# Output projection of a pooling and convolution layer: the pool half as four groups of seven block products, and the pool map moved into the input projection

## The reference, cut to what matters

```python
proj = h @ w_in                      # 2048 -> 4096: u | B | C | v, 1024 each
u, bg, cg, v = ...
ya, new_pool = _pool_mixer(pool_prev, u, pos0, w_pool, pool_scale)
#   per group g (256 channels, window 2/4/8/16):
#   d = mean over the window - u;  y = (d @ w_pool[g]) * pool_scale
yb, new_conv = _conv_mixer(conv_prev, bg, cg, v, conv_w)     # B * conv3(C * v)
x = x + jnp.concatenate([ya, yb], axis=-1) @ w_out           # 2048 -> 2048
x = x + _cross_attn(...)             # 4 heads over 256 memory tokens
x = x + square(relu(rms(x) @ w_up)) @ w_down
```

## Time and profile before

| what | value |
|---|---|
| median of 3 runs | 2573.04 us (2572.37 to 2573.59) |
| the profiled execution | 2572.41 us, of it span 2570.7 us |
| PE busy | 2542.2 us, 99% of the span, 19628 matmuls |
| DVE busy | 2018.9 us, 79% |
| ACT busy | 1162.8 us, 45% |
| share of PE in the chain that ended last | 90% |
| share of DVE in it | 6% |
| granted TensorE clock | 0.998 of full speed |

### The profile page before, as it was taken

How to read it: one execution, slowest core, us unless ns; L and a number is a source line. 1 busy time by engine, 2 the same in 40 slices (tenths; PEclk the granted TensorE clock), 3 DMA queues, 4 the chain that set the end, 5 groups by cost and what they waited for, 6 DMA issues and landing times.

```text
span 2570.7 us, 46979 instructions
## 1 busy us (share of the span) xinstructions
PE 2542.2 (99%) x19628; PEld 2476.8 (96%) x19628; DVE 2018.9 (79%) x2510; ACT 1162.8 (45%) x1616; POOL 174.7 (7%) x278
## 2 busy tenths in 40 slices
PE   8999999999999999999999999999999999999998
PEld 7889999999999979899999999999999999999997
DVE  8898888763686663478888888888888888888888
ACT  6445444441453341245555555666543333333344
POOL 1000000010000020000111110000010000000000
PEclk9999999999999999999999999999999999999999
DMA  8663333362334385433566665555586565556532
GB/s 306 208 206 123 108 106 110 118 221 87 132 125 161 123 323 206 172 117 109 178 223 220 225 222 212 195 190 206 203 306 219 192 227 209 208 191 224 195 129 103
DMA packets 134499, 471.44 MB, mean 183 GB/s; under 512 B 12544, under 2 KB 18816, under 8 KB 123040
## 3 DMA queue, kind: packets, MB, share of 16 engines
q1 hardware_dynamic: 92224, 259.74, 30.4%
q0 software_dynamic: 41664, 208.62, 21.9%
q10 hardware_dynamic: 416, 0.30, 0.0%
HBM read 381.08 MB, written 87.54 MB: 182 GB/s over the span
## 4 chain that ended last, share of the span: by engine, by line
PE 90%; DVE 6%; issue 2%; ACT 2%; DMA 1%; DVEq 0%; ACTq 0%; POOL 0%; POOLq 0%; SPq 0%
PE psum_main L2915 27%; PE psum_side L2915 20%; PE psum_main L2501 14%; PE psum_main L2629 10%; PE psum_side L2629 8%; PE psum_main L2605 3%; PE psum_main L2558 2%; DVE unit_low L2159 1%; PE psum_main L2839 1%; PE psum_main L2767 1%; PE psum_main L2560 1%; DMA unit_raw<-weights 1%; ACT unit_high L1335 1%; PE psum_side L2808 1%; PE psum_side L2708 1%
## 5 line engine op out<-in xcount | busy, mean ns | idle before, releaser
L1335 ACT ACTIVATE unit_high<-unit_raw 128x1024 fp32r<-128x1024 f32 x382 | 398.6, 1055 | 520.2 <-PE psum_main L2915 159.0
L2159 DVE TENSOR_TENSOR unit_low<-unit_raw,unit_high 128x1024 fp32r<-128x1024 f32 x382 | 465.5, 1222 | 101.7 <-ACT unit_high L1335 101.5
L2915 PE MATMUL psum_main<-tokens_late,unit_high 128*128 128x272 f32 x2048 | 388.5, 288 | 2.0 <-DVE hidden L2261 1.0
L2915 PE MATMUL psum_main<-hidden,unit_high 128*128 128x272 f32 x1984 | 376.8, 288 | 0.7 <-DVE residual_late L2293 0.7
L2915 PEld LDWEIGHTS psum_main<-tokens_late,unit_high 128*128 128x128 f32 x2048 | 321.9, 189 | 2.6 <-DVE hidden L2261 1.5
L2915 PEld LDWEIGHTS psum_main<-hidden,unit_high 128*128 128x128 f32 x1984 | 312.2, 189 | 1.1 <-DVE residual_late L2293 0.9
L2915 PE MATMUL psum_main<-tokens_late,unit_low 128*128 128x272 f32 x1024 | 295.1, 288 | 0.0
L2915 PE MATMUL psum_side<-tokens_late,unit_high 128*128 128x272 f32 x1536 | 293.1, 288 | 1.5 <-issue 0.8
L2629 PE MATMUL psum_main<-tokens,unit_high 128*128 128x272 f32 x1536 | 292.1, 288 | 0.9 <-DVE pool_lines L1713 0.7
L2915 PE MATMUL psum_main<-hidden,unit_low 128*128 128x272 f32 x992 | 286.1, 288 | 0.0
L2915 PE MATMUL psum_side<-hidden,unit_high 128*128 128x272 f32 x1488 | 283.6, 288 | 0.0
(11 more groups left out here) (339 smaller groups left out, 5044.8 us busy)
## 6 DMA issues: line engine op xcount, KB each, us to landing
unit_raw<-weights SPq DMA_DIRECT2D x436, 512.0 KB, 4.3
hidden<-hidden_kept POOLq DMA_DIRECT2D x56, 1088.0 KB, 5.7
hidden_kept<-hidden_staged POOLq DMA_DIRECT2D x31, 1904.0 KB, 7.4
unit_sum<-weights SPq DMA_DIRECT2D x44, 512.0 KB, 3.6
residual<-x_t POOLq DMA_DIRECT2D x16, 544.0 KB, 7.0
residual_kept<-residual_new POOLq DMA_DIRECT2D x32, 272.0 KB, 2.3
cache_ring_q<-cache_k POOLq DMA_DIRECT2D x8, 1024.0 KB, 5.9
cache_low_a<-cache_v POOLq DMA_DIRECT2D x8, 1024.0 KB, 10.8
```

What stands on the lines that cost most here:

```text
L1335: act.activation(WHI[:, slot, :], raw, ACT.Copy).then_inc(mlp_high, 1)
L2159: dve.tensor_tensor(WLO[:, slot, :], raw, WHI[:, slot, :].bitcast(F32), ALU.subtract) \
L2915: ins = pe.matmul(bank, w[:, slot, col:col + P], moving[:, k, part, :], start=start and k == 0 and n == 0, stop=k == kk - 1 and n == 2, sk ...
```

## The change

- **The pool half of the output projection** becomes four quads, 16 to 19 (`OUT_QUADS`), of seven products each, with the pool rows as the token side. One product is again 24 matmuls (2 output blocks x 4 inner blocks x 3). Results are not copied: seven DVE additions into X per quad (`add_out`). The quads take their raw blocks as halves of stored units, so each block is two DMAs with 128 numbers (512 bytes) in a run.
- **The token side** of these products needs seven combinations of the pool rows. They are made group by group inside the input projection (`mix_parts`, `low_raw_parts`, `low_mixed_parts` on DVE, `high_raw_parts`, `high_mixed_parts` on ACT), written to DRAM (`parts_kept`) and read back as `PAIRS` into the places of the token operands that quad 15 frees. The last group's are made inside quad 15 and written directly (`high_last_part`, `low_part`).
- **The pool map** of each group runs on PE right behind the value quad (`map_pool`, 24 matmuls), from operands that ACT and DVE split there (`high_differences`, `high_map`, `low_differences`, `low_map`); its results are scaled by ACT in the gate quad (`map_scaled`).
- **The conv rows** keep only two rows on chip (`Y`), are stored per group (`y_kept`) and come back late for the conv half (`high_rows`, `low_rows`).
- Slots of later stages are renumbered, since 18 units leave the ring; the first loads of quad Q0 and of the MLP's quad 0 are issued in another order.

The diff, cut:

```diff
-    ("pool_map", 2,  8,  8, 0, 0,  0),
-    ("pool_out", 16, 16, 0, 0, 0,  0),
+    ("pool_map", 0,  0,  8, 0, 0,  0),
-SLOT_OF = (2, 3, 0, 1, 2, 3, 0)
+SLOT_OF = (0, 1, 2, 3, 0, 1, 2)
+OUT_QUADS = 4
-Q0 = MIX_QUADS
+Q0 = MIX_QUADS + OUT_QUADS
+OUT_ROWS = ((10, 12), (4, 6), (0, 2), (14, 8))
...
@@ SP
+            def load_block(q, tile, w, landed):
+                if not MIX_QUADS <= q < Q0:
+                    sp.dma_start(tile, w).then_inc(landed, 16)
+                else:
+                    for u in range(2):
+                        sp.dma_start(tile[:, u * 512:u * 512 + 512].rearrange("p (g n) -> p g n", g=HK), w[u]) \
+                            .then_inc(landed, 16)
...
@@ POOL
+                if g:
+                    store_parts(g - 1, 3, PRODUCTS, MIXED_PARTS)
+                    store_rows(g - 1)
...
+            for i in range(PRODUCTS):
+                pool.wait_ge(in_used, in_use(last_mix, i // 2))
+                pool.dma_start(PAIRS[i // 2][:, i % 2, 0:3, :, :]..., parts_kept[PART_AT[i]]...)
...
@@ ACT, in the loop over the mixing quads
                 high_in(q, 5)
+                if kind(q) == "pool":
+                    high_mixed_parts(g - 1)
+                if kind(q) == "value":
+                    high_differences(g)
                 act.wait_ge(in_dve, 3 * q + 1)
                 copy_in(q, 3, 0, S[:, 2, 0:HALF])
+                if kind(q) == "value":
+                    high_map(g)
+                if q == MIX_QUADS - 1:
+                    act.wait_ge(mixed, PARTS_MIXED)
+                    high_last_part(PAIRS[1][:, :, 3, 0, :], 1, halves(DIFF[:, 0, :]))
+                    high_last_part(PAIRS[2][:, 0, 3, 0, :], 2, DIFF[:, 1, HALF:TOK])
+                    high_last_part(PAIRS[3][:, 0, 3, 0, :], 3, DIFF[:, 1, 0:HALF])
                 high_in(q, 6)
...
@@ DVE, in the same loop
                 sum_in_4(q)
+                if kind(q) == "pool" and g:
+                    mix_parts(g - 1)
+                if kind(q) == "gate" and g < 3:
+                    low_raw_parts(g)
+                if q == MIX_QUADS - 1:
+                    low_part(done + 1, PAIRS[0][:, :, 3, 1, :], ...)
...
                 low_in(q, 5)
+                if kind(q) == "value":
+                    low_differences(g)
+                if kind(q) == "pool" and g:
+                    low_mixed_parts(g - 1)
+                if q == MIX_QUADS - 1:
+                    low_part(done + 2, ...)
+                    mix_parts(g)
                 low_in(q, 6)
+                if q == MIX_QUADS - 1:
+                    low_part(done + 3, ...)
+                    low_part(done + 4, ...)
+                    low_part(done + 5, ...)
...
+                sum_in_1(q + 1)
+                if q:
+                    block_out(q, 2)
+                low_in(q + 1, 0)
+                if kind(q) == "value":
+                    low_map(g)
+                block_out(q, 3)
...
@@ DVE, quads 16 to 19
+                add_out(q, 3)
+                low_in(q, 6)
+                if q + 1 < Q0:
+                    sum_in_1(q + 1)
+                add_out(q, 4)
+                if q > MIX_QUADS + 1:
+                    for n in range(4):
+                        low_rows(4 * (q - MIX_QUADS - 2) + n)
...
@@ PE
+            def product_out(q, i, out, start):
+                pe.wait_ge(in_ready, in_use(q, i))
+                for m in range(2):
+                    for k in range(HK):
...
+                        for n, (w, part) in enumerate(((WHI, 0), (WHI, 1), (WLO, 0))):
+                            ins = pe.matmul(out[:, m, :], w[:, slot, col:col + P], PAIRS[i // 2][:, i % 2, k, part, :], ...)
+            for q in range(MIX_QUADS, Q0):
...
+                pe.wait_ge(in_dve, done + 1)
+                product_out(q, 2, chain_out(q), False)
...
-            down("pool_out", A, ready_by(psum_free, lambda k: s0["tiles"] + max(5, k + 1)), apart=True)
-            down("conv_out", B, ready_by(y_split, lambda k: k + 1))
+            down("conv_out", B, None, apart=True)
```

More of the change, by code:

```diff
@@ L480, in first_half @@
         def first_half(q, row):
[L482 removed]
             at_line = lambda t, pad: t[:, row, pad:pad + HALF]
[L484 removed]
+            return {"pool": at_line(U, PAD), "content": Y[:, row, 0:HALF], "value": at_line(Z, CPAD),
                     "gate": GATE[:, row, 0:HALF]}[kind(q)]
@@ new lines, in load_map, with store_parts @@
+            def load_map(g):
+                if g:
+                    pool.wait_ge(map_high, 3 * g)
+                    pool.wait_ge(map_ready, 3 * g)
+                pool.dma_start(MAP_RAW[:, :], weights[MAP_IN + g // 2][:, g % 2 * 512:g % 2 * 512 + 512]) \
+                    .then_inc(map_loaded, 16)
+            def store_parts(g, first, last, made):
+                pool.wait_ge(stage_ready, GROUP_PARTS * g + made)
+                pool.dma_start(parts_kept[first:last, :, g].rearrange("i p s n -> p i (s n)"),
+                               PARTS_OUT[:, 0:last - first, :, :].bitcast(F32).rearrange("p i s n -> p i (s n)")) \
+                    .then_inc(parts_stored, 16)
@@ new lines, in _ @@
+            pool.wait_ge(stage_high, PARTS)
+            pool.wait_ge(stage_ready, PARTS)
+            load_x(2)
+            load_x(3)
+            store_rows(3)
+            load_x(0)
+            load_x(1)
+            load_x(7)
+            for n in range(2):
+                pool.wait_ge(k_stored[n], KEYS_STORED + 16 * 4)
+            load_x(4)
+            for n in range(2):
+                pool.wait_ge(in_used, in_use(last_mix, 4 + n))
+                pool.dma_start(B[:, 4 * n:4 * n + 4, 1, :].bitcast(F32),
+                               y_kept[4 * n:4 * n + 4].rearrange("k p n -> p k n")).then_inc(y_back[n], 16)
@@ L1154, in _ @@
-            for c in range(CH):
-                act.wait_ge(y_made, c + 1)
-                act.activation(B[:, c, 0, :], Y[:, c, :], ACT.Copy).then_inc(y_high, 1)
+            for n in range(RING):
+                convert_first(n)
             def down(name, extra=0, groups=4):
@@ L1707, in block_out @@
                     dve.wait_ge(pool_kept, 2 * g + 2)
-                if kind(q) == "gate":
-                    dve.wait_ge(k_stored[row], KEYS_STORED + 16 * (g + 1))
+                if kind(q) == "gate" and g:
+                    dve.wait_ge(y_made, 2 * g)
+                if kind(q) == "content" and g:
+                    dve.wait_ge(k_stored[row], KEYS_STORED + 16 * g)
                 def add(out, a, b):
@@ L1721, in block_out @@
                 elif half:
-                    out = (Y[:, 2 * g + row, :] if kind(q) == "content" else GATE[:, row, :])[:, HALF:TOK]
+                    out = (Y if kind(q) == "content" else GATE)[:, row, HALF:TOK]
                     add(out, bank, part).then_inc(in_dve, 1)
@@ L2529, in down @@
                 if apart:
-                    for j in range(2):
-                        multiply(unit(name, extra, j), j, tiles, 0, True, True, ready if j == 0 else None)
                     group(0, (2, 3))
@@ L2701, in keys_of_caches @@
+            for j in range(2):
+                pe.wait_ge(in_dve, dve_reads(Q0 - 1 + j))
+                multiply(unit("conv_out", 0, j), j, B, 0, True, True, (lambda k: pe.wait_ge(y_split, k + 1)) if j == 0 else None)
+            down("conv_out", B, None, apart=True)
             def keys_of_caches(h, n):
```

563 lines of the change are left out of this document (335 added, 228 removed).

## The result

The changed kernel takes **2587.9 us** (median of 4 runs, 2587.5 to 2588.5) against 2572.7 us (4 runs) of the kernel before on the same chip: ratio 1.006, 95% interval 1.0048 to 1.0071. It is 15 us slower, where 2569.2 us was forecast and the range ended at 2579.5. The span of the profiled execution is 2586.8 us (2570.7 before).

The account below looks back on a forecast made before the run. PE, busy 99% of the span, was taken to bound the kernel; 13.4 us removed against 9.6 us of new waits gave 3.8 us faster, from 2573.04 to 2569.2 us, range 2562.5 to 2579.5.

Parts of the forecast that it names:

- PE's list: Map and pool half on PE: 13.4 us removed, 12.0 from 96 matmuls fewer and 1.4 from waits in the old stage.
- value quads: Quads 2, 6, 10, 14: product 6 waits for block_out, 1.4 us in group 0, 0.5 in group 1; sum 1.9.
- pool quads: Quads 4, 8, 12: mixing on DVE delays block_out, so product 6 waits 0.5 us, three times 1.5 us in all.
- gate quads 3, 7, 11: The parts' low halves come ahead of the taps; taken as nothing, with 0.5 us each as upper bound.
- quad 15: DVE's list: Last parts, mixing and low halves ahead of block_out(15, 2) make product 6 of quad 15 wait 5.0 us.
- quad 16: list: DVE's queue after quad 15 makes product 2 wait 0.6 us and product 4 wait 0.1; sum 0.7.
- quads 16 to 19: weights: Waits for weight blocks in the output quads: 0.5 us in all.
- load term: Weight loads in output quads: nothing up to twice the 4.3 us landing; 0.5 us in all taken.
- rival 2: Output quads wait for weights at sum_in_1 in quads 16 to 18: 10.5 us instead of 0.5, 2579.2 us; chance 0.11.
- The mixing: Pool quads: four DVE operations, each waiting for the last, 0.47 us apart, 1.8 us; 1.4 by the Trainium skill's page.
- the 12 that the prediction named as its sign: PE waiting more than 12 us in all between 230 and 560 us would mean the forecast is too fast.
- rival 3: Content quads of groups 1 to 3 wait for stored conv rows, 1.6 us each: 2574.0; chance 0.12 including other waits.

Follow-up runs that it names:

- i: Changed kernel with each weight block of the output quads stored as one unit, one 512 KB transfer with 4 KB a row: 2574.5 us.
- k: As i, one transfer a block, but the two blocks of a pair of units stored interleaved, so runs are 512 bytes again: 2588.4 us.
- f_best: Changed kernel with a, b and the order of d in every quad: 2573.3 us.
- e_all: Changed kernel with the edits of a, b and d together: 2578.4 us.
- d: Changed kernel; in quad 15 ACT rounds operand 6 before the last parts, DVE does block_out(15, 2) right behind low half 6: 2589.2 us.
- m: Changed kernel with the seven loads of the parts read in runs of 544 bytes, as two transfers each: 2592.9 us.
- b: Changed kernel with the loads of residual and conv rows each behind a product of its own in quads 17 to 18: 2578.7 us.
- a: Changed kernel with the seven loads of the parts spread over nine products instead of four: 2579.4 us.
- c: Changed kernel with the output quads' blocks in the same two halves but in runs of 2 KB (other weights): 2581.1 us.
- g: e_all with the output quads' blocks read in the 2 KB runs of c (other weights): 2572.5 us.
- j: f_best with the whole stored blocks of i: 2566.1 us.
- l: As j, without the spreading of parts and rows (a and b): 2568.1 us.

## Why the prediction was wrong

Counted at the first conv addition; each forecast is the prediction's, each measured number from the profiled execution:

| Term | forecast us | measured us |
|---|---|---|
| PE's list | -13.4 | -13.4 |
| start of the first quad | 0 | +1.2 |
| value quads | +1.9 | +2.4 |
| pool quads | +1.5 | +2.9 |
| gate quads 3, 7, 11 | 0 | +0.9 |
| quad 15: DVE's list | +5.0 | +5.4 |
| quad 15: weights | 0 | +3.3 |
| quad 15: slow clock | 0 | +1.7 |
| quad 16: list | +0.7 | +0.4 |
| quads 16 to 19: weights | +0.5 | +10.1 |
| quad 16: slow clock | 0 | +2.0 |
| not placed | | +1.0 |
| sum | -3.8 | +17.9 |

**The step that failed** is the load term, "Bounds: nothing, if it takes up to twice 4.3, and rival 2 above. ... I take 0.5 us in all, near the lower end, as both rows are". It measured 13.4 us of waits (3.3 + 10.1). The slow clock behind the waits cost 3.7 more; the part in quad 15 (1.7) would largely be there without the late weights too: behind the wait of 5.3 in i, product 6 still takes 4.45 us instead of 3.0 (549.57 to 554.02 us).

Three things in it were wrong. The landing time was taken from rows of quiet stretches and doubled at most; it became 14.2 us for half a block. The only place looked at was quads 16 to 18, while the first late block is the one of quad 16 that is loaded in quad 15, beside the parts. And the row held against rival 2, that 1 KB runs cost 0.3 us more, says nothing of the weights' queue: it is two loads on POOL's queue, and there the runs of 1 KB travel in packets of 4.1 KB (115 packets with 0.47 MB from 958 to 960 us before, with no weights beside them). On SP's queue each run of 512 bytes is a packet.

Against rival 2 stood also a rule of the Trainium skill, page "DMA: Bandwidth & Descriptors", section "Specifications": 512 bytes is the least run for the full rate. The trace does not agree. Nearly alone on full engines (98% of the bytes from 549 to 553 us are the weights'), the runs of 512 bytes move 299 GB/s; alone in the kernel before, in runs of 4 KB, the weights reach 385 (windows, after and before):

```profile
549.00:553.00 4.00, 0.00 (x0) 0.00 (x0) 0.85 (x1) 0.00 (x0) 1.45 (x2) 0.50 1.18 299
307.00:309.00 2.00, 2.00 (x18) 2.00 (x18) 1.91 (x5) 0.33 (x2) 0.00 (x0) 1.00 0.97 385
```

The sum of 410 GB/s from 538 to 548 us is no support for the rule, since 92% of those bytes are in POOL's long packets. And beside these the queue with the short runs gets still less, 32 GB/s. That decided (2588.4 us against 2574.5, k and i).

**Rival 2** is what came true, at a price of 13.4 us where 10.5 had been worked out: 3.3 one quad sooner and 10.1 in quad 16 alone, not 3.5 in each of three quads. Quads 17 and 18 had no such wait. Its deciding point, 9.4 us per block, was passed where even half a block took 14.2. Its chance of 0.11 was too small: the bytes that quad 15 asks for are in the code, seven parts of 816 KB in 21 us (278 GB/s), four blocks of 512 KB (100) and two residual loads of 544 KB (53), 431 GB/s in all, more than the 400 to 420 that the engines move when full.

**What held.** PE's list: a product takes 3.01 us and a piece of the map 3.01, as worked out, so its -13.4 stand in the table unchanged (of the 1.4 us that it laid on waits in the old stage the trace names 0.8). The waits named, their places and releasers: value quads 1.2 and 0.6 (forecast 1.4 and 0.5), pool quads three times 0.7 (0.5), quad 15's list 5.4 (5.0). The mixing went as the earlier trace rows led to expect, four operations 0.47 to 0.48 apart (timeline of DVE, pool quad of group 1), not 0.35:

```profile
293.34 0.44 DVE L1942 TENSOR_TENSOR pool_differences<-pool_differences 128x272 f32<-128x272 f32 x1
293.82 0.44 DVE L1944 TENSOR_TENSOR pool_differences<-pool_differences 128x272 f32<-128x272 f32 x1
...
295.25 1.23 DVE L1799 TENSOR_TENSOR unit_low<-unit_raw,unit_high 128x1024 fp32r<-128x1024 f32 x1
```

PE's waits between 230 and 560 us came to 12.6 us, past the 12 that the prediction named as its sign. Quads 17 to 19 had no wait in their lists, and rival 3 (stored rows late) did not occur.

**What was small and one-sided.** Each of the five short waits costs 0.3 us more than it is long: product 6 behind it takes 3.29 us instead of 3.00. And product 5 of the gate quads takes 3.23 instead of 3.01, where the earlier trace rows has even pace, without a wait that the view names (chain of waits, after: start us, us, what):

```profile
254.31 3.29 PE psum_main L2825 x24
...
275.72 3.23 PE psum_side L2825 x24
...
587.38 8.08 PE psum_main L2894 x48
```

The start of the first quad, 191.47 us against 190.29 before, seems not to be the change's: it lies behind a stage that is the same in both, and the profiled executions of f_best and i, which have the change too, have 190.21 and 190.82. Without the weights' trouble the forecast would still have been some 5 us too fast, as i_whole_blocks shows (2574.5 against 2569.2): 0.3 us for each restart, the gate quads, and a slow clock after 5.3 us of waiting. That split is argued from the table, not tried one by one. f_best comes nearest: without the five waits it is 5.1 us below e_all, though it changes the order in the other quads too.

## What to carry to other kernels

Before a landing time from a quiet stretch is used, add up the bytes that all queues want in the new place, in GB/s, and set them beside the highest rate that the trace shows. Where they meet it, look at each queue's packet size: here the queue with the short packets was the one that starved, and a layout that makes its blocks contiguous can be worth more than all reordering. An order that only brings the next wait forward gives nothing (d); take away what ends last first.

## What the runs showed of the hardware

- Where two queues of one core shared full engines, they took turns packet by packet: 643 to 640, and 727 to 727, packets in 10 us; cut into single us, from 538 to 548 us the two counts never differ by more than 4 in the changed kernel. At 512 bytes against 5.8 KB the weights had 8% of the bytes. Such a packet itself took its engine 0.027 us (10.7% of 16 x 10 us over 640), 19 bytes a ns, against 25.7 for POOL's (0.227 us). So a short run costs about a quarter of the engine's rate, which the 299 GB/s show when it is nearly alone, and beside long packets it costs much more, its share of the turns.
- Over longer stretches the counts are not equal (723 to 1527 from 572 to 582 us): from 574 to 576 us they are 178 to 178, from 576 to 578 us 87 to 840. That POOL's queue had little to move in those 2 us (0.31 MB) is likely, but the trace does not show what a queue holds.
- Packets are not always runs: POOL's queue carried runs of 544 bytes in packets of 3.7 KB (m) and runs of 1 KB in packets of 4.1 KB (before), SP's queue runs of 512 bytes in packets of 0.5 KB.
- SP can be held in the issue of a transfer: 8.65 us from 538.14 us on, in the chain of waits of quad 15, while the engines were full. The blocks behind it are late before they begin. The longest issues are 8.4 to 9.9 us in the kernels with runs of 512 bytes and the parts not spread (changed kernel, b, d, k, m), 1.2 to 3.8 with the parts spread (a, e_all, f_best), 1.4 and 1.1 with runs of 2 KB (c, g), and 0.33 with runs of 4 KB (i, j, l), though the engines of i were as full. So the hold comes with the short runs; by what SP was held the trace does not say, and how much of the lateness is the hold and how much the turns no run parts.
- All DMA engines of the core together moved at most some 425 GB/s over 10 us (424 from 1080 to 1090 us in the changed kernel, 427 in j).
- Behind waits of 8.7 and 10.1 us PE first ran at the granted clock of 0.50 (1.2 GHz) and lost another 1.7 and 2.0 us. Behind the one of 5.3 us in i it did so too: 0.66 over the window from 548 to 553 us, pairs of matmuls of 0.65 us.
